# Convolution blocks ahead of the gate blocks, and each group's turn five output blocks sooner, in one decoder step on one core

## The reference

```python
def mamba_layer(x, ...):                       # 64 heads in 8 groups
    proj = rmsnorm(x, norm_g) @ w_in
    z, xbc, dt_raw = split(proj)               # gate, convolution input, time step
    xbc = silu(causal_conv(xbc))               # 4 taps per channel; the old rows come from conv_prev
    xs, Bm, Cm = split(xbc)
    y, s = ssd_chunk_scan(xs, softplus(dt_raw + dt_bias), -exp(A_log), Bm, Cm, s_prev)
    y = (y + xs * D_skip) * silu(z)
    y = rmsnorm_per_group(y) * gate_norm
    return x + y @ w_out, conv_new, s
```

## Time and profile before

| | |
|---|---|
| median of 3 runs | 2434.68 us (2434.57 to 2435.46) |
| profiled execution | 2432.4 us, its span 2430.6 us |
| PE busy | 2238.6 us, 92% of the span |
| DVE / ACT / POOL busy | 1330.0 / 1143.2 / 1103.7 us |
| first input block of group 0 to the end of group 7's last output block here | about 63 to 956 us |

### The profile page before, as it was taken

How to read it: one execution, slowest core, us unless ns; L and a number is a source line. 1 busy time by engine, 2 the same in 40 slices (tenths; PEclk the granted TensorE clock), 3 DMA queues, 4 the chain that set the end, 5 groups by cost and what they waited for, 6 DMA issues and landing times. The chain is left out here.

```text
span 2430.6 us, 39422 instructions
## 1 busy us (share of the span) xinstructions
PE 2238.6 (92%) x13958; PEld 1912.0 (79%) x13958; DVE 1330.0 (55%) x2181; ACT 1143.2 (47%) x2863; POOL 1103.7 (45%) x718
## 2 busy tenths in 40 slices
PE   3999999999999998789998985999999999999689
PEld 2998999889998987689996763777777767777489
DVE  3557666666666666533125655665565655665410
ACT  4355455555455555543344443554444545544332
POOL 1655656555655664256772222633333332333066
PEclk7999999999999999799998896999999999999889
DMA  2565656464646465234442212212112122021444
GB/s 97 193 222 171 209 180 219 165 228 169 222 167 226 167 208 172 96 117 145 152 161 90 108 45 83 59 30 64 35 59 61 30 60 66 23 69 54 192 138 145
DMA packets 80349, 309.83 MB, mean 127 GB/s; under 512 B 14578, under 2 KB 21874, under 8 KB 54690
## 3 DMA queue, kind: packets, MB, share of 16 engines
q1 hardware_dynamic: 80162, 307.38, 37.6%
HBM read 279.56 MB, written 27.79 MB: 126 GB/s over the span
## 5 line engine op out<-in xcount | busy, mean ns | idle before, releaser
L632 POOL TENSOR_TENSOR w_lo<-raw,w_hi 128x1024 fp32r<-128x1024 f32 x218 | 536.7, 2483 | 381.9 <-ACT w_hi L816 362.8
L122 PE MATMUL bank<-h_hi,w_hi 128*128 128x304 f32 x1936 | 600.7, 310 | 24.3 <-POOLq L251 13.8
L124 PE MATMUL bank<-h_hi,w_lo 128*128 128x304 f32 x1936 | 587.8, 304 | 0.0
L123 PE MATMUL bank<-h_lo,w_hi 128*128 128x304 f32 x1936 | 585.2, 302 | 0.0
L122 PEld LDWEIGHTS bank<-h_hi,w_hi 128*128 128x128 f32 x1936 | 366.9, 190 | 36.8 <-issue 14.6
L122 PE MATMUL bank<-b_hi,a_hi 128*128 128x512 f32 x896 | 362.2, 404 | 28.3 <-issue 16.1
L816 ACT ACTIVATE w_hi<-raw 128x1024 fp32r<-128x1024 f32 x216 | 216.6, 1050 | 355.9 <-PE bank L124 355.9
L123 PEld LDWEIGHTS bank<-h_lo,w_hi 128*128 128x128 f32 x1936 | 367.9, 190 | 2.4 <-issue 1.7
L124 PEld LDWEIGHTS bank<-h_hi,w_lo 128*128 128x128 f32 x1936 | 367.1, 190 | 0.0
L124 PE MATMUL bank<-b_hi,a_lo 128*128 128x512 f32 x896 | 354.9, 396 | 0.0
L123 PE MATMUL bank<-b_lo,a_hi 128*128 128x512 f32 x896 | 354.9, 396 | 0.0
(11 more groups left out here) (364 smaller groups left out, 3774.7 us busy)
## 6 DMA issues: line engine op xcount, KB each, us to landing
raw<-in_a_units SPq DMA_DIRECT2D x112, 1024.0 KB, 5.0
raw<-in_b_in_units SPq DMA_DIRECT2D x20, 1024.0 KB, 4.8
past<-in_cache SPq DMA_DIRECT2D x64, 288.0 KB, 3.2
s_in<-in_state_in SPq DMA_DIRECT2D x32, 512.0 KB, 6.5
s_t<-in_state_t SPq DMA_DIRECT2D x16, 1024.0 KB, 6.6
out_state_out<-s_in SPq DMA_DIRECT2D x32, 512.0 KB, 6.9
pt<-in_cache_t SPq DMA_DIRECT2D x64, 256.0 KB, 2.6
raw<-in_o_units SPq DMA_DIRECT2D x16, 1024.0 KB, 5.3
```

The source lines that it names most:

```text
L122: nc.tensor.matmul(out, a[0], b[0], start=start, stop=False)
L123: nc.tensor.matmul(out, a[0], b[1], start=False, stop=False)
L124: return nc.tensor.matmul(out, a[1], b[0], start=False, stop=stop)
L632: nc.gpsimd.tensor_tensor(w_lo[u % 2][:, c], raw[u % 2][:, c], w_hi[u % 2][:, c].bitcast(F32), ALU.subtract).then_inc(lo_done, 1)
```

## The change

`mamba_blocks` puts the six convolution blocks of groups 1 to 7 ahead of the four gate blocks (group 0 had them so already), and the weight units are laid out in that order. DVE convolves c0 to c3 in the slots 2 to 5 in place of 5 to 8, and B and C in the slots 6 to 9 in place of one tap behind each of the first eight output blocks. The pieces of `start` come five output blocks sooner. In the last group `heads(7, 0)` to `heads(7, 2)` stand behind the output blocks 11, 13 and 15 on PE and DVE. SP's code is unchanged. The lines of the new file are 1 to 3 higher.

```diff
-        blocks += [(kind, g, k) for kind, k in z + c] + [("o", g - 1, c_) for c_ in range(KT)]
+        blocks += [(kind, g, k) for kind, k in c + z] + [("o", g - 1, c_) for c_ in range(KT)]
...
+    LATE = (11, 13, 15)
...
             def start(g, c):                       # TensorE
-                if c == 6:
+                if c == 2:
                     x_turned(g)
                     samples_turned(g)
+                if c == 4:
+                    b_and_c(g)
                 if c == 9:
-                    b_and_c(g)
-                if c == 14:
                     of_states(g, 0)
-                if c == 15:
+                if c == 10:
                     update(g, 0)
...
+                    if g == GROUPS - 1 and c in LATE:
+                        heads(g, LATE.index(c))
-            for k in range(IN_UNITS):
+            for k in range(len(LATE), IN_UNITS):
                 heads(GROUPS - 1, k)
...
             def start(g, c):                       # VectorE
-                if c < 4:
-                    conv(g, xB, (c,))
-                elif c < 8:
-                    conv(g, xC, (c - 4,))
-                elif c < 11:
-                    if c == 8:
-                        samples_back(g)
-                    x_back(g, c - 8)
+                if c == 3:
+                    samples_back(g)
+                if 3 <= c < 6:
+                    x_back(g, c - 3)
...
-                    if 5 <= k < 9:
-                        conv(g, k - 5)
+                    if 2 <= k < 6:
+                        conv(g, k - 2)
+                    elif k >= 6:
+                        conv(g, (k - 6) // 2 + xB, ((0, 1), (2, 3))[k % 2])
...
-        units += [tile(w[:, c:c + P]) for c in (gates + conv if g else conv + gates)]
+        units += [tile(w[:, c:c + P]) for c in conv + gates]
```

More of the change, by code:

```diff
@@ L498, in mamba_stage @@
     for n, (kind, g, k) in enumerate(blocks):
-        u = unit_at(g) + at[kind, g, k] - at["z" if g else "c", g, 0] if kind != "o" else unit_at(g + 1) + IN_UNITS + k // 4
+        u = unit_at(g) + at[kind, g, k] - at["c", g, 0] if kind != "o" else unit_at(g + 1) + IN_UNITS + k // 4
         last_of_unit[u] = n
@@ L650, in in_block @@
                 n = at[kind, g, k]
-                u = unit_at(g) + n - at["z" if g else "c", g, 0]
+                u = unit_at(g) + n - at["c", g, 0]
                 bank_free(n)
@@ L784, in start @@
             def start(g, c):
-                if c == 6:
+                if c == 2:
                     x_turned(g)
                     samples_turned(g)
+                if c == 4:
+                    b_and_c(g)
                 if c == 9:
-                    b_and_c(g)
-                if c == 14:
                     of_states(g, 0)
-                if c == 15:
+                if c == 10:
                     update(g, 0)
             for g in range(GROUPS):
-                for k, b in enumerate(blocks[at["z" if g else "c", g, 0]:][0:IN_UNITS if g else CONV_BLK]):
+                for k, b in enumerate(blocks[at["c", g, 0]:][0:IN_UNITS if g else CONV_BLK]):
                     in_block(*b)
@@ L920, in _ @@
                 first = IN_UNITS if g else CONV_BLK
-                of_g = blocks[at["z" if g else "c", g, 0]:][0:IN_UNITS]
+                of_g = blocks[at["c", g, 0]:][0:IN_UNITS]
                 for k in range(first):
@@ L1101, in start @@
             def start(g, c):
-                if c < 4:
-                    conv(g, xB, (c,))
-                elif c < 8:
-                    conv(g, xC, (c - 4,))
-                elif c < 11:
-                    if c == 8:
-                        samples_back(g)
-                    x_back(g, c - 8)
-                if c == 9:
[L1111 to L1118, removed]
+                if c == 3:
+                    samples_back(g)
+                if 3 <= c < 6:
+                    x_back(g, c - 3)
+                if c == 5:
+                    c_spread(g)
+                if c == 6:
+                    cb_back(g)
+                if c == 7:
+                    b_back(g)
+                if c == 8:
+                    b_spread(g)
+                if c == 9:
                     skip(g, 0)
                     skip(g, 1)
-                if c == 15:
+                if c == 10:
                     skip(g, 2)
```

## The result

The changed kernel takes 2509.3 us (median of 4 runs, 2505.3 to 2510.3) against 2434.7: a ratio of 1.0306, with a 95% interval of 1.0291 to 1.032. The forecast was 2486 us in a range of 2448 to 2513. The sign is right and the time in the range, but of the 74.6 us that were lost the sum has 51. The profiled execution took 2505.3 us, 72.9 more than the one before.

What follows compares the result with a forecast made beforehand. PE was taken to bound the loop, with about 1.4 us idle per repetition. Losses 25.2 + 8.4 + 15 + 4 - 1.7 = 51 us on the profiled 2432.4, plus 2.3 for the median, gave 2486 us; range 2448 to 2513.

Steps and rivals of the forecast that it cites:

- the second rival: Input slots 3 to 5: convolutions meet POOL's low parts, DVE stops PE some 5 us per group; 2517 us, chance 0.10.
- Part 2: Start pieces among the output blocks: PE waits for b_and_c and s_t, 2.15 us in each of seven groups, 15 us.
- Part 3: DVE in the input blocks: the mixing for pair_y(2) in slot 5 ends 0.6 us late per group, 4 us.
- Part 1: Groups 2 to 7: block 2 waits 4.2 us for c0's evacuation, which waits for conv_old; 25.2 us.
- the first and the third rival: First: conv_old lands in time, 2452 us, chance 0.10. Third: start pieces find everything ready, 2424 us, chance 0.07.
- The clock: Behind each of the six conv_old waits: one fall and return of PE's clock, 1.4 us each, 8.4 us.
- Part 4: Behind the loop: pieces moved among output blocks 10 to 15 shorten an 18.7 us stretch to 17.0, 1.7 us won.

Runs made afterwards that it cites:

- one unit sooner: Changed kernel with conv_old issued in the same input block but ahead of that block's unit on SP: 2476.8 us.
- the run that takes these waits away: Changed kernel with DVE's last two taps of C and the conv_new copies ahead of the scaling of y in the last input slot: 2489.8 us.
- the run with the short low part: Changed kernel with POOL computing only 64 of 1024 columns of each half of one unit's low part in groups 1 to 7: 2488.6 us.
- the staggered kernel: The kernel without the staggering, plus the last group's DVE updates and mixings, PE pieces and ACT's second decay put behind different blocks: 2430.1 us.
- the kernel without the staggering: Changed kernel with conv_old early, C's last taps ahead of the scaling, B and C's silu ahead of the split, s_t one unit sooner: 2437.4 us.
- the silu: Changed kernel with ACT's silu of B and C directly behind that of x, ahead of the split that waits for output block 3: 2511.1 us.
- conv_old early: Changed kernel with SP issuing a group's conv_old eight input blocks into the group before: 2475.0 us.

## Why the prediction was right, and where it was short

The sign and the main wait were foreseen; that the time lies in the range is in part luck. 2509.3 is 4 us under the upper end, and nearer to the second rival's 2517 than to the forecast's 2486. A loss of 19.5 us was not in the sum at all, and two terms that came out smaller than forecast (Part 2's waits by 3.4, Part 3 by 4) hid some of it.

- **Part 1, the wait for conv_old (25.2 us): right.** 27.3 us in six waits; in group 7 4.00 against 4.2, with the landing at 6.65 against 6.8. No more was lost behind ACT's split: PE waits for no low part in the loop. (The wait came four blocks sooner and not five, and `x_turned` four output blocks sooner; no number rests on it.) With this landing the first and the third rival fall. The Trainium skill (DMA: Bandwidth & Descriptors, "Anatomy of one DMA") gives an estimate of 2.2 us for these 72 KB, by a fit made for transfers that GpSimd issues; from SP they took 6.6 in the median at this place and 4.7 one unit sooner.
- **The clock (8.4): mis-sized, and its upper bound was wrong.** One case of 1.4 us was taken for the price and for the bound. The input halves lost 38.8 us, of which 27.3 are waits: 11.5 for six falls, 1.3 to 2.6 each. The two longest waits, 5.4 and 5.6 us, were followed by the two largest losses, 2.5 and 2.6; the four of 4.0 to 4.2 by 1.3 to 1.8.
- **Part 2, the start pieces (15): its two waits near, 8.3 for `b_and_c` against 10.2 and 3.4 for s_t against 4.9.** The step that failed is the rule that it worked by: "the question for each moved piece is what releases it now". That asks what a moved piece waits for, and not who stands behind it. C's last taps were moved to DVE's last input slot; behind them stand the additions, which did not move, and behind those PE's output block 2. This cost 16.3 us of waits and two falls of the clock, 3.2 by the block starts (5.1 against 3.5): 19.5 (the run that takes these waits away won 19.5 as well), of the 23.6 that the sum is short.
- **Part 3, DVE (4): `pair_y` does not wait in the loop (both waits of the 7.9 us, 3.73 and 4.17, are behind it), so 0.** The second to fourth taps were slowed, 956 to 1306 ns in the mean (the first ones went from 1612 to 1083), but group 1's input half takes 83.0 us as before. The second rival had the right mechanism, exclusion by POOL, at the wrong place: not in the slots 3 to 5 but at the seam between slot 9 and output block 0. The Trainium skill (SBUF — State Buffer, "Who interferes with whom") says that the loser is fully blocked; the run with the short low part agrees for the taps, and also for the copy, which has one SBUF input (0.16 us without the low part, 2.33 with it).
- **Part 4, behind the loop (-1.7): about 0.** Group 7's output half and what follows lost 3.7 us, of which 2.33 and 1.17 are the waits above. A gain was there to be had, if not the 10.7 of the bound: the staggered kernel takes 75.1 us for this stretch, 5.2 less than the kernel before and 7.2 less than the kernel without the staggering. In the changed kernel DVE's update and PE's next products stood behind the same output block, so PE waited 2.63 and 1.63 us; behind the first of these it ran at a mean clock of 0.69 from 1026.0 to 1030.0, behind the second at 1.00.
- The rest, some 4 us, is not traced in full: 1.0 comes before group 1, which no step touches, and small delays of the start pieces may be the other 3 (output halves of 34.3 us with the waits mended, against 33.9).

## What to carry to other kernels

For each piece that is moved ask two things: what it waits for in its new place, and what, on the same engine, now waits behind it, above all what hands a buffer back to the engine that sets the time. A wait that is taken away is worth only the distance to the next one (the silu: 0, until s_t was moved too), so follow the chain to the piece behind it before pricing it. And where two dependent pieces on two engines are put behind the same block, look for a stall of about the first one's length (here 2.63 and 1.63 us for an update of 2.15): putting the producer a block sooner took it away.

## What the runs showed of the hardware

- The same idle of PE is not followed by the same clock. Behind a wait of 2.33 us (and 0.44 one block earlier) the granted clock stayed at 1.00, the level of 2.4 GHz, in five groups of the changed kernel, and in two it fell for a while to the level of 1.2 GHz (0.50 from 230 to 232 us, 0.67 in the mean of the 5.1 us of that stretch). With PE's waits for conv_old gone it fell in six of seven groups (conv_old early) and in seven of seven (one unit sooner). Each count is from one profiled execution. So the price of a wait can rise when another one is taken away, here by some 6 us in the program. What decides is not settled.
- A copy of 128x24 floats, one input and one output in SBUF, took 2.33 us on DVE beside POOL's low part and 0.16 without it.
- The same 72 KB from the same queue landed in 6.6 us (median) where a unit and two more transfers were issued in the 1.3 us ahead of them, and in 4.7 where one unit was issued 0.4 us ahead.
